# Two late key tiles, a z tile and a gate tile moved around the first score rows of a latent attention, in a fp32 kernel of two models in a row

## The reference

```python
qm = (rmsnorm(mq, mla_q_norm) @ mla_w_uq).reshape(B, S, MLA_HEADS, MLA_QK)
kv = (rmsnorm(mkv, mla_kv_norm) @ mla_w_ukv).reshape(B, S, MLA_HEADS, MLA_NOPE + MLA_DV)
q_pe = apply_rope(qm[..., MLA_NOPE:], cos, sin)
k_pe = apply_rope(mkr[:, :, None, :], cos, sin)
...
# causal_block_attention, one block of 128 queries
s = jnp.einsum('bhqd,bhkd->bhqk', qi, k).astype(jnp.float32) * scale
s = jnp.where(kpos[None, :] <= qpos[:, None], s, -jnp.inf)
p = jax.nn.softmax(s, axis=-1).astype(v.dtype)
return jnp.einsum('bhqk,bhkd->bhqd', p, v)
...
o_a = rmsnorm(o_a, gdn_out_norm) * silu(gz)     # delta rule's output
o_b = causal_block_attention(...) * silu(mz)    # attention's output
```

## Time and profile before

| what | value |
|---|---|
| runs | 2119.32, 2119.20, 2115.18 us, median 2119.2 |
| profiled execution, own time | 2117.37 us |
| its span | 2115.4 us, mean granted TensorE clock 0.972 |
| busy: PE / PE weight loads | 2017.3 us (95%) / 1523.0 us (72%) |
| busy: DVE / ACT / POOL | 1255.8 us (59%) / 917.8 us (43%) / 648.8 us (31%) |
| DMA | 174.26 MB, mean 82 GB/s |
| a weight chunk of 512 KB, issue to landing | median 3.2 us |
| chain that ended last | PE 73%, DVE 21%, ACT 3%, issue 2%, DMA 1% |

### The profile page before, as it was taken

The page is one execution under the profiler, slowest core; times in us unless marked ns, Lnnn a source line. Parts: engine busy times, 40 slices in busy tenths (PEclk is TensorE's granted clock), DMA queues, the critical chain, the costliest instruction groups (busy, mean ns, idle before and its releaser), DMA issues.

```text
span 2115.4 us, 28250 instructions
## 1 busy us (share of the span) xinstructions
PE 2017.3 (95%) x10992; PEld 1523.0 (72%) x10992; DVE 1255.8 (59%) x1986; ACT 917.8 (43%) x1482; POOL 648.8 (31%) x308
## 2 busy tenths in 40 slices
PE   8999999999999999999899999899999999989997
PEld 6667874657667786467777787677777868867776
DVE  4688945456679874555648765545234777464432
ACT  4432245333442235343347437445234753554531
POOL 2323431223323332033334312223533432222252
PEclk9999999998999999999899999899999999989998
DMA  6223221142231232131322101112232210111232
GB/s 228 85 91 119 84 101 50 60 139 80 101 122 61 103 112 70 42 128 60 111 84 90 39 15 46 60 50 95 96 114 89 90 58 15 37 59 51 72 106 81
DMA packets 47858, 174.26 MB, mean 82 GB/s; under 512 B 5646, under 2 KB 6286, under 8 KB 46320
## 3 DMA queue, kind: packets, MB, share of 16 engines
q1 hardware_dynamic: 47600, 172.34, 24.0%
q10 hardware_dynamic: 128, 0.13, 0.0%
HBM read 157.77 MB, written 14.68 MB: 82 GB/s over the span
## 4 chain that ended last, share of the span: by engine, by line
PE 73%; DVE 21%; ACT 3%; issue 2%; DMA 1%; DVEq 0%; ACTq 0%
PE bank L628 14%; PE bank L637 13%; PE bank L642 12%; PE bank L745 4%; PE bank L757 2%; PE bank L1171 2%; PE bank L1151 2%; PE bank L828 1%; PE bank L673 1%; PE bank L842 1%; PE bank L905 1%; DVE arena L1968 1%; DVE arena L1972 1%; PE bank L765 1%; DVE arena L1970 1%
## 5 line engine op out<-in xcount | busy, mean ns | idle before, releaser
L2531 POOL TENSOR_TENSOR w_lo<-wraw,w_hi 128x1024 fp32r<-128x1024 f32 (+2 forms) x248 | 590.4, 2382 | 1325.3 <-ACT w_hi L1241 1325.3
L1241 ACT ACTIVATE w_hi<-wraw 128x1024 fp32r<-128x1024 f32 (+2 forms) x248 | 253.0, 1020 | 688.1 <-PE bank L642 429.8
L628 PE MATMUL bank<-h_hi,w_hi 128*128 128x512 f32 x1568 | 410.9, 404 | 6.8 <-DVE arena L2258 5.6
L637 PE MATMUL bank<-h_lo,w_hi 128*128 128x512 f32 x1568 | 389.4, 390 | 0.2
L642 PE MATMUL bank<-h_hi,w_lo 128*128 128x512 f32 x1536 | 379.5, 389 | 0.0
L628 PEld LDWEIGHTS bank<-h_hi,w_hi 128*128 128x128 f32 x1568 | 294.7, 191 | 98.6 <-issue 31.8
L637 PEld LDWEIGHTS bank<-h_lo,w_hi 128*128 128x128 f32 x1568 | 295.1, 188 | 64.3 <-DVE h_lo L1807 1.6
L642 PEld LDWEIGHTS bank<-h_hi,w_lo 128*128 128x128 f32 x1536 | 288.3, 188 | 59.8
L745 PE MATMUL bank<-arena,wdir 128*128 128x512 f32 x256 | 114.7, 599 | 1.2 <-DMA wdir<-in_w_direct 1.2
L2004 DVE CUSTOM_DVE_ANT_0 arena<-bank,arena 128x512 f32<-128x512 f32 x64 | 44.2, 691 | 89.7 <-PE bank L828 88.4
L2437 DVE TENSOR_TENSOR bank<-bank,con 128x128 f32<-128x128 f32 x64 | 19.2, 299 | 129.1 <-PE bank L1157 128.1
(11 more groups left out here) (403 smaller groups left out, 3192.7 us busy)
## 6 DMA issues: line engine op xcount, KB each, us to landing
wraw<-in_w_split SPq DMA_DIRECT2D x220, 512.0 KB, 3.2
wdir<-in_w_direct SPq DMA_DIRECT2D x16, 512.0 KB, 3.9
x_park<-arena SPq DMA_DIRECT2D x3, 2048.0 KB, 6.2
arena<-x_park SPq DMA_DIRECT2D x3, 2048.0 KB, 7.8
wraw<-in_w_split SPq DMA_DIRECT2D x12, 384.0 KB, 3.1
hg_park<-arena SPq DMA_DIRECT2D x2, 2048.0 KB, 8.7
arena<-hg_park SPq DMA_DIRECT2D x2, 2048.0 KB, 8.1
wraw<-in_w_split SPq DMA_DIRECT2D x16, 256.0 KB, 2.6
```

The costliest lines, as they stand in the source:

```text
L628: mm(ps[0:wd, 0:S], hi[:, k, :].bitcast(F32R), h_hi[:, k, :].bitcast(F32R), start=k == 0 and not begun, stop=False)
L637: ins = mm(ps[0:wd, 0:S], hi[:, k, :].bitcast(F32R), h_lo[:, k, :].bitcast(F32R), start=False, stop=bool(parts) and k == KT - 1)
L1241: a(w_hi[:, n % 2, 0:f].bitcast(F32R), wraw[:, n % 2, 0:f], ACT.Copy).then_inc(hi_done, 1)
L2531: nc.gpsimd.tensor_tensor(w_lo[:, n % 2, 0:f].bitcast(F32R), wraw[:, n % 2, 0:f], w_hi[:, n % 2, 0:f], ALU.subtract).then_inc(lo_done, 1)
```

## The change

Behind the scan kn 4 and kn 5 are made after vv 7, ahead of the first scores. Rows 0 and 1 carry kn 6 and kn 7, row 2 mz 0, row 3 gz 0; rows 4 and 10 carry nothing any more. ACT takes over vv 4 ahead of the squares and vv 5 behind them, then cuts only the first rotated query, takes the root, takes over vv 6 and vv 7, cuts the second query, takes over kn 4 and kn 5, and loads the exp table last. The queries of heads 2 to 7 are cut by ACT at the end of rows 0 to 5. On DVE only `turned_lo(0)` stands ahead of the reciprocal; those of heads 1 to 7 stand at the end of rows 1 to 7. PE waits for "qn" 7 and no longer for vv 7 ahead of the scores, and `mvalues` waits for its value tiles.

```diff
--- before.py
+++ after.py
@@ -94,8 +94,9 @@
     BESIDE_LATENT[NT * _h] = [("mz", _h - 1)]
 for _h, _n in enumerate((10, 18, 22, 26)):
     BESIDE_LATENT[_n] = [("gz", _h)]
-for _n in range(4):
-    BESIDE_LATENT[_n] = [("kn", 4 + _n)]
+BESIDE_LATENT[0], BESIDE_LATENT[1] = [("kn", 6)], [("kn", 7)]
+BESIDE_LATENT[2], BESIDE_LATENT[4] = [("mz", 0)], []
+BESIDE_LATENT[3], BESIDE_LATENT[10] = [("gz", 0)], []
 BESIDE_STATE = [[("kn", n)] if n < 4 else [("vv", n - 4)] for n in range(NC_)]
 TURN_AT = {1: "vN", 2: "kN"}
 RS_AT = 6
@@ -160,6 +161,7 @@
             jobs += [("su", l, ck, p) for p in range(2)] if ck < NC_ - 1 else []
             jobs += [(g, l, j) for g, j in BESIDE_STATE[ck]]
         jobs += [("vv", l, 4), ("vv", l, 5), ("on", l), ("vv", l, 6), ("vv", l, 7)]
+        jobs += [("kn", l, j) for j in range(4, 6)]
         todo = [(h, i) for h in range(MH) for i in range(NT)]
         for n, (h, i) in enumerate(todo):
             jobs += ([("ms", l, h, i), ("ms", l, *todo[1])] + [("nb", l, j) for j in range(H)] if n == 0 else [])
@@ -1137,6 +1139,8 @@
                 row_sums(("on", l), [onsq[:, h, :] for h in range(H)], [("on_sq", l, h) for h in range(H)])
                 values_tile(6)
                 values_tile(7)
+                for j in range(4, 6):
+                    tile("kn", j)
 
                 def head_norm(h):
                     ps = take("nb", l, h)
@@ -1166,6 +1170,7 @@
 
                 def mvalues(h):
                     ps = take("mo", l, h)
+                    pe.wait_ge(*read("vv", l, 2 * (h // 2) + 1))
                     pe.wait_ge(*read("mt", l, h, NT - 1))
                     for kb in range(NT):
                         ins = mm(ps[:, kb * P:S], vn[:, h, kb * P:(kb + 1) * P], PT[:, h % 2, kb, kb * P:S],
@@ -1173,7 +1178,7 @@
                     ins.then_inc(filled("mo", l, h), 1)
 
                 todo = [(h, i) for h in range(MH) for i in range(NT)]
-                pe.wait_ge(*read("vv", l, MH - 1))
+                pe.wait_ge(*read("qn", l, MH - 1))
                 mscores(*todo[0])
                 mscores(*todo[1])
                 for h in range(H):
@@ -1694,8 +1699,10 @@
                             keep((g, l, j), kn[:, j, :])
                     if ck in ROTATED_AT:
                         turn_queries(ROTATED_AT.index(ck))
+                keep_values_tile(4)
                 for h in range(H):
                     a(onsq[:, h, :], oa[:, h, :], ACT.Square).then_inc(up("on_sq", l, h), 1)
+                keep_values_tile(5)
 
                 def turned_hi(h):
 
@@ -1708,14 +1715,13 @@
                 act.wait_ge(*after("qr_sb", l, 3))
                 act.wait_ge(*read("vn", l, NC_ - 1))
                 turned_hi(0)
+                row_root(("on", l), row_q, P)
+                keep_values_tile(6)
+                keep_values_tile(7)
                 turned_hi(1)
-                turned_hi(2)
-                turned_hi(3)
-                row_root(("on", l), row_q, P)
+                for j in range(4, 6):
+                    keep(("kn", l, j), kn[:, j, :])
                 link(a(small[:, 60:61], small[:, 4:5], ACT.Exp))
-                for h in range(4, MH):
-                    keep_values_tile(h)
-                    turned_hi(h)
                 todo = [(h, i) for h in range(MH) for i in range(NT)]
                 msc = float((P + ROPE) ** -0.5)
 
@@ -1748,6 +1754,8 @@
                     for g, j in BESIDE_LATENT[n]:
                         keep((g, l, j), {"mz": zm, "gz": zg, "kn": kn}[g][:, j, :])
                     mkeep(h, i)
+                    if n < MH - 2:
+                        turned_hi(n + 2)
                     if i == 0 and h:
                         keep_values(h - 1)
                     if 8 <= n < 12:
@@ -2415,8 +2423,7 @@
                 link(v.tensor_tensor(kr_parts[0:ROPE, 1, :].bitcast(F32R), kr[0:ROPE, :], kr_parts[0:ROPE, 0, :], ALU.subtract))
                 v.tensor_tensor(kr_parts[ROPE:P, 2, :].bitcast(F32R), kr[ROPE:P, :], kr_parts[ROPE:P, 0, :],
                                 ALU.subtract).then_inc(up("kr_lo", l), 1)
-                for h in range(6):
-                    turned_lo(h)
+                turned_lo(0)
                 dve.wait_ge(*read("on", l))
                 link(v.reciprocal(row_q, row_q))
                 link(v.tensor_copy(rows[:, 0, :].bitcast(F32R), row_q))
@@ -2457,8 +2464,8 @@
                     if n < 2:
                         norm_head(2 * n)
                         norm_head(2 * n + 1)
-                    if n in (4, 5):
-                        turned_lo(n + 2)
+                    if 0 < n < MH:
+                        turned_lo(n)
                     if 10 <= n < 14:
                         dve.wait_ge(*after("oc_hi", l, n - 10))
                         v.tensor_tensor(oc_rest[:, n - 10, :].bitcast(F32R), oc[:, n - 10, :], oc_hi[:, n - 10, :],
```

## The result

The changed kernel took 2124.55 us (median of 8 runs, 2123.00 to 2126.71), the kernel before 2117.66 us in 8 runs beside it (2115.18 to 2119.32). The ratio is 1.0032 with a 95% interval of 1.0023 to 1.0042: **6.9 us slower**, 4.9 to 8.9. Forecast was +3.8 us on the median of the first three runs (2123.0), in a range of 2115 to 2128. Every one of the 8 runs is slower than every run of the kernel before. The profiled execution has a span of 2121.7 us, 6.3 more than before.

The account below looks back on a forecast made before the run. PE, busy 95% of the span, was taken as the bound, so only its idle time and slow clock could change. Per layer +2.2 +0.7 -1.0 = +1.9 us, +3.8 in two, on a median of 2119.2: 2123.0, range 2115 to 2128.

Parts of the forecast that it names:

- Part 1: ACT and DVE up to nb: the cast waits for POOL's weight rest; nb starts at 1326.2, before 1327.78.
- Part 2: PE up to row 2's first tile: slow clock after idle time, then DVE; mz 0 starts at 1336.4, before 1337.64.
- Then DVE bounds: From row 2's mask to the first full tile DVE sets the pace: 6.27 us less 0.71 idle, 5.56.
- Part 3: Rows 2 to 4 with gz 0 take 16.5 us, 0.8 waiting in row 4; row 5's scores come 2.2 later.
- Part 4: Rows 5 to 8: `turned_lo` in row 6 stands ahead of row 7's `mweigh`, +0.7 us a layer.
- Part 5: Rows 9 to 12 lose gz 0 but gain only 1.0 us, with idle time and slow clock like rows 13 to 16.
- Rival B: Faster: cast not held up, clock stays up; 2117.4 us, or 2114.1 with clock up in rows 9 to 12; chance 0.17.
- list of signs: What would show the forecast, including 3.6 us idle before nb and row 5's scores about 34.8 us behind vv 7.
- case A: The forecast itself: moved tiles fill one hole and open another, +3.8 us, 2123.0; chance 0.45.
- C: Slower: idle time around head 1's first scores lowers the clock and mz 0 pays; 2126.3 us, chance 0.35.
- D: The change fails to do what it says: mz 0's weights late in row 2; chance 0.03.

Follow-up runs that it names:

- e5: Changed kernel with mz 0's weights cut by ACT behind row 1's exponentials, not at kn 5's takeover: ratio 1.0009 to the kernel before.
- e1: Changed kernel with the exp table loaded ahead of the takeover of kn 4 and kn 5: ratio 1.0020 to the kernel before.
- e4: Changed kernel with row 1's scores made five times over to fill PE's idle time ahead of nb: ratio 1.0003 to the kernel before.
- e2: Changed kernel with DVE's `turned_lo` of heads 1 to 7 at the end of rows 0 to 6, not 1 to 7: ratio 1.0010 to the kernel before.
- e3: Changed kernel with gz 0 back in row 10, row 3 carrying no tile: ratio 1.0008 to the kernel before.
- e10: Kernel before with only its tiles spread (mz 0 to 3 in rows 4, 6, 10, 14, gz 0 in 8): ratio 0.9974 to the kernel before.
- e8: Changed kernel with the edits of e5 and e2, mz 0 to 3 in rows 2, 6, 10, 14, gz 0 in 4: 2103.9 us, ratio 0.9934.
- e9: Changed kernel with only the tiles spread (mz 0 to 3 in rows 2, 6, 10, 14, gz 0 in 4): ratio 0.9987 to the kernel before.
- e11: e8 with row 1's scores made three times over in the idle time ahead of nb: 2104.8 us, ratio 0.9944 to the kernel before.

## Why it came out this way, step by step

**Part 1 was right.** The reciprocal was to start at 1320.15 and started at 1319.90; POOL's rest was to run from 1322.6 to 1325.0 and ran from 1322.80 to 1325.14; the cast was to end at 1325.3 and ended at 1325.42; nb was to start at 1326.2 and started at 1326.35. e5 shows what the collision costs in nb's time: 1.70 us in the first layer, 1.36 in the second. The Trainium skill ("SBUF — State Buffer", section "SBUF: two separate sides") has GpSimd and a VectorE operation that takes their shared ports lock each other out for a whole instruction, the first to start being first served. The casts of 2.13 and 1.78 us agree, and e1 shows both orders: 2.79 us for DVE where POOL was 0.10 ahead, 2.71 us for POOL where DVE was 0.26 ahead.

**Part 2 failed in one term**, "Then DVE bounds: ... it has 6.27 us, less 0.71 idle, 5.56". From the mask of row 2 to `turned_lo(1)` DVE took 1336.72 - 1329.97 = 6.75 us, 1.08 of them idle: it waited for the scores of row 3, which PE makes behind kn 6, and kn 6 ran at half clock to its end. The forecast took the idle time out as if the clock were back by then. But the row it used has the same wait in the same place, 0.71 us behind a slow kn 4; it was no time to be saved. mz 0 started at 1337.8, forecast 1336.4: 1.4 us a layer, of which 1.2 are this term. e4 shows it from the other side: with the clock up, mz 0 starts 2.5 us earlier.

**Part 3 was right**: 16.81 us, forecast 16.5; the wait on ACT in row 4 0.85, forecast 0.8.

**Part 4 was right in its wait and wrong in its price.** PE waits 0.91 in row 7 in place of 0.38. But the slow spell was longer: 18.36 us, clock 0.81 against 0.90. +1.6 where 0.7 was forecast, 0.5 of it idle time and 1.1 busy. That the longer wait brings the longer spell isn't shown: e2 waits 1.10 there and has a clock of 0.90.

**Part 5 was wrong in the other direction.** The waits came as described (1.50 and 0.99, together 2.49; I named 1.4 and 1.1), but the clock stayed at 1.00: -2.65 where -1.0 was forecast. e2 has these rows at 16.61 with the same waits, so this term is 1.0 or 2.65 as it falls. (Rival B's price for half clock, "about 1.65", doesn't follow from its own numbers, 16.59 - 2.6 - 12.11 = 1.88; e2 measures 1.65, because the other matmuls take 12.48 beside such waits and not 12.11. In the list of signs, the row-5 scores by Parts 1 to 3 are 34.5 us behind vv 7, not 34.8.)

**The sum**: forecast +2.2, +0.7, -1.0 a layer; the profile has +3.8, +1.6 and -2.65, together +2.8, and +3.0 in the second layer. The waits of the mechanism were all there. The mis-sized thing is one: I priced slow clock from the rows of before at their places, and it is neither fixed to a place nor to a length.

That the time came within 1.6 us of the forecast is in part luck. The stretch of Parts 1 to 3 was 1.6 us a layer too low, Part 4 0.9 too low and Part 5 1.65 too high, which cancels most of it. And the forecast stood on a median of three runs (2119.2) that was 1.5 above that of eight (2117.66): as a difference it is 6.9 us where 3.8 was forecast. The outcome beyond 0.2% had a chance of 0.40, the one within it 0.43.

The forecast case A holds for the waits; by its time the result lies between A (2123.0) and C (2126.3), whose mechanism the changed kernel itself didn't show: mz 0 ran at full clock. Rival B is out as a whole: in every layer in which the cast met POOL's rest, nb came 12.96 to 13.01 us behind the row sums. Its second step, the clock staying up in rows 9 to 12, did come about. D is out: mz 0's weights were never waited for.

What stays open: how much of the 6.9 us is systematic and how much is the way in which slow spells happen to lie in this kernel. e3, e5 and e2 each gained 4.7 to 5.1 us on the changed kernel, where their waits explain 2 to 3.4 and the intervals reach 2 us to each side; summed they are more than the loss. So the waits are shown one by one, but the 6.9 us can't be shared out among them.

## What to carry to other kernels

Count waits by rows of a schedule before moving a tile: here full tiles in rows 10 and 12 hid all waits of rows 9 to 12; three bare rows in succession left 2.9 us (17.62 to 14.97, a tile of 5.51 gone) where the clock stayed up and 4.5 where it fell; and spreading five tiles won 6 us by itself (e10). With the change and two mends it was 13 (e8), but without the mends under 3 (e9). When an operation moves in time, look at what GpSimd and VectorE do beside each other at the new time; a move by another microsecond may only make it a race (e1), and the safe mend orders the two by a dependence (e5). Even that only chooses what the long operation meets instead (e5, e11), so check that too. Filling a hole keeps the clock up only to the next wait (e4, e11). And an operation that only one consumer needs soon belongs in the idle time of the producer before it (e2), not at the end of a busy row.

## What the runs showed of the hardware

The same instructions with the same waits (2.1 and 0.38 us, 2.49 in all) took 16.61 us in one kernel's rows 13 to 16 and 14.95 in another's, with a granted clock of 0.90 and 1.00. The part of the program ahead of the seam is the same code in all kernels, but the row sums of the first layer began at 1312.28 us in e2 and at 1315.58 in e5. So differences under some 3 us between two single profiles of this kernel say nothing by their spans, and ten executions of one kernel (e2) spread over 6.5 us with their mean clock. The waits repeat better: the one ahead of row 6's transposes was 2.22 us in both layers of all nine kernels that have rows 5 to 7 bare. Not all do: the wait in row 7 lay between 0.33 and 1.10.

VectorE and GpSimd hold each other up in many places of this kernel. Beside a weight rest of 1024 columns (2.34 to 2.44 us) a cast of 512 columns took 2.13 and 1.78 in place of 0.43, a scaling of 384 columns 2.25 in place of 0.42 (row 2 of the changed kernel, hidden behind mz 0), and a difference of two SBUF tiles 2.03 in place of 0.69 (e9). A reciprocal of 512 columns took its 3.35 us beside a rest of 512 columns that took its usual 1.27 (kernel before).
